# Matrix-LSTM heads in spans of 256 tokens with a chained state, on one core

## The chip, the core and the metric

One core of a Trainium2 chip runs the program. TensorE (PE; PEld is its weight load) multiplies, VectorE (DVE), ScalarE (ACT) and GpSimd (POOL) work on elements, SyncE (SP) issues the loads of weights. The metric is the device time of one execution in microseconds (us).

## The reference

One decoder layer for 1024 tokens, width 1024, all float32. Its first part runs two groups of heads on one input projection, sparse attention (NSA, 8 heads) and the matrix LSTM (mLSTM, 4 heads of 128), then projects both back and adds them to `x`. Cross attention and a gated MLP follow. The change lies in the mLSTM heads:

```python
def step(carry, inp):                       # chunks of 64 tokens
    C, n, m = carry
    qq, kk, vv, ii, lf = inp
    b = jnp.cumsum(lf, axis=-1)
    D = jnp.where(causal, b[..., :, None] - b[..., None, :] + ii[..., None, :], -jnp.inf)
    m_inter = b + m[..., None]
    m_t = jnp.maximum(jnp.max(D, axis=-1), m_inter)
    a_inter = jnp.exp(m_inter - m_t)
    sc = jnp.einsum('bhtd,bhsd->bhts', qq, kk) * jnp.exp(D - m_t[..., None])
    num = a_inter[..., None] * jnp.einsum('bhtd,bhde->bhte', qq, C) + jnp.einsum('bhts,bhse->bhte', sc, vv)
    den = a_inter * jnp.einsum('bhtd,bhd->bht', qq, n) + jnp.sum(sc, axis=-1)
    h = num / jnp.maximum(jnp.abs(den), jnp.exp(-m_t))[..., None]
    ...
```

`q` and `k` come from a causal convolution of four taps and a SiLU; `h` is normalized by head and multiplied by a sigmoid gate `o`.

## The kernel before

Products of float32 matrices are made of three matmuls on split operands (high by high, low by high, high by low: `product`, lines 1066 to 1070). GpSimd splits each 128-column weight tile (`w_hi` L882, `w_lo` L887) once TensorE has begun the tile before, into two slots that take turns. `gemm_tile` projects one tile over 1024 tokens in two halves of 512, each into one of the eight banks of PSUM; a ring gives out the banks as chunks in order, and `open_chunk` waits until the chunk seven before it has been taken out (`chunk_freed`).

After attention come the four mLSTM heads. A head's order on TensorE: projection of q; transposes of the head before (`turn_head`, which waits for `hm_ready`); projections of k, v and the gate; transposes of v (`mv_feat`); the scores of all 36 causal pairs of 128-token blocks in twelve `pieces` of up to 512 columns; in head 3 also the 32 transposes of the attention output `o_nsa`; then the products with v, 1 to 8 for each block of tokens (L1342), into numerator and denominator (129 columns).

VectorE takes q out, convolves it (L2557 to L2562), splits it after ScalarE's SiLU (L2259), multiplies the gate of the head before (L2546), does the same for k, takes v out (L2576), makes the masked exponents of the eight diagonal blocks (L2583), takes the gate out (L2586) and v's tokens (L2589), multiplies each piece of scores by its decay (L2601, L2606; the exponentials are ScalarE's, L1865), takes out the outputs (L2621, L2622) and normalizes the head (L2626 to L2634), which ends in `h_mls`. In head 3 it also makes the low parts of the attention output and of heads 0 to 2 in `h_hi`/`h_lo`, all ahead of the outputs.

Then `mixed` begins the output projection with the first two weight tiles over both token halves; for k from 4 on (the mLSTM heads) it waits for `split_ready`. `turn_head(3)` stands behind 18 groups of three matmuls. Each engine does its instructions in the order of the code.

## Time and profile before

| what | value |
|---|---|
| runs | 1744.65, 1744.93, 1745.40 us, median 1744.93 |
| the profiled execution | span 1742.3 us from first to last instruction |
| busy | TensorE 97%, its weight loads 81%, VectorE 71%, GpSimd 51%, ScalarE 42% |
| mean granted TensorE clock | 0.987 |
| mLSTM heads | 448.5 to 696.1 us of the span |

The page gives the span of one profiled execution and no longer time of it. Matmuls are pipelined: a record's duration is longer than its distance from the next one, so the distance between starts is what a product costs. A float32 product is two records. Columns of instructions in order of time: start, duration, engine, line, operation, output and inputs, shape, count, and in brackets the idle time before with what released it.

### The profile page before, as it was taken

How to read it: one execution, taken by the hardware profiler on the slowest of the kernel's cores; microseconds unless marked ns; L12 is line 12 of the kernel's file. 1: busy time of each engine (PE TensorE's matmuls, PEld its weight loads, DVE VectorE, ACT ScalarE, POOL GpSimd, SP SyncE). 2: the span in 40 equal slices, each digit the busy share in tenths (PEclk: the TensorE clock that was granted, in tenths of full speed). 3: DMA queues.
4: the chain of work that ended last, by engine and by line, in shares of the span. 5: the costliest groups of instructions: out<-in, count | busy, mean ns of one | idle time of the engine just before them, and what ended most of it. 6: DMA issues, size and time to landing. Idle time of an engine off the chain costs nothing.

```text
span 1742.3 us, 23240 instructions
## 1 busy us (share of the span) xinstructions
PE 1682.1 (97%) x8496; PEld 1406.2 (81%) x8496; DVE 1229.0 (71%) x1654; ACT 729.4 (42%) x1367; POOL 881.1 (51%) x671
## 2 busy tenths in 40 slices
PE   7998899998999999999999999999999999999997
PEld 6886788887788888889888787878888888877886
DVE  6764578776777877546554535878888878789965
ACT  5113577876233134115332314343444444443444
POOL 3342345443422421430412544379988788779841
PEclk9999899999999999999999999999999999999999
DMA  5230111110111113224201142234543454685332
GB/s 197 68 103 25 49 33 29 34 29 25 45 41 37 59 38 109 97 97 159 84 25 36 49 145 86 78 121 164 188 157 127 139 167 148 246 297 174 126 124 97
DMA packets 80334, 176.51 MB, mean 101 GB/s; under 512 B 7836, under 2 KB 24412, under 8 KB 80096
## 3 DMA queue, kind: packets, MB, share of 16 engines
q1 hardware_dynamic: 67944, 135.71, 23.5%
q10 hardware_dynamic: 12280, 39.34, 6.0%
q8 instruction: 68, 1.11, 0.3%
q14 instruction: 42, 0.34, 0.1%
HBM read 136.21 MB, written 38.81 MB: 100 GB/s over the span
## 4 chain that ended last, share of the span: by engine, by line
PE 56%; DVE 15%; POOL 12%; ACT 8%; issue 8%; DMA 1%; ACTq 0%; SPq 0%; POOLq 0%; DVEq 0%
PE ps L1066 13%; PE ps L1070 13%; PE ps L1069 13%; DVE x_t L2845 4%; PE ps L1260 3%; POOL sum_s L977 2%; ACT x_t L2086 2%; PE ps L1342 2%; POOL w_lo L971 2%; POOL w_lo L1027 2%; PE ps L1231 2%; PE ps L1281 2%; PE ps L1282 1%; DVE x_t L2874 1%; PE ps L1232 1%
## 5 line engine op out<-in xcount | busy, mean ns | idle before, releaser
L1066 PE MATMUL ps<-h_hi,w_hi 128*128 128x512 f32 x1060 | 418.3, 395 | 8.1 <-POOL h_lo L955 3.2
L1069 PE MATMUL ps<-h_lo,w_hi 128*128 128x512 f32 x1060 | 413.9, 390 | 0.0
L1070 PE MATMUL ps<-h_hi,w_lo 128*128 128x512 f32 x1060 | 413.8, 390 | 0.0
L882 POOL TENSOR_TENSOR w_hi<-w_raw,ones 128x1024 fp32r<-128x1024 f32 x52 | 109.3, 2101 | 516.3 <-PE ps L1066 433.5
L1066 PEld LDWEIGHTS ps<-h_hi,w_hi 128*128 128x128 f32 x1060 | 199.5, 188 | 57.4 <-ACT p_sum L2055 8.5
L1070 PEld LDWEIGHTS ps<-h_hi,w_lo 128*128 128x128 f32 x1060 | 199.5, 188 | 42.2
L1069 PEld LDWEIGHTS ps<-h_lo,w_hi 128*128 128x128 f32 x1060 | 199.6, 188 | 39.6
L915 POOL TENSOR_SCALAR probs<-probs,nsa_inv,gate_sig 128x640 f32<-128x640 f32 (+7 forms) x128 | 100.3, 783 | 178.6 <-DVE nsa_inv L2462 178.6
L2845 DVE SCALAR_TENSOR_TENSOR x_t<-ps,par,x_t 128x1023 f32<-128x1023 f32 x84 | 107.7, 1282 | 72.7 <-ACT x_t L2086 71.2
L2258 DVE TENSOR_TENSOR pt_lo<-ps,pt_hi 128x512 fp32r<-128x512 f32 (+1 forms) x148 | 101.7, 688 | 59.3 <-ACT pt_hi L1796 57.4
L887 POOL TENSOR_TENSOR w_lo<-w_raw,w_hi 128x1024 fp32r<-128x1024 f32 x52 | 139.6, 2685 | 4.0
L1796 ACT ACTIVATE pt_hi<-ps 128x512 fp32r<-128x512 f32 (+1 forms) x148 | 87.8, 596 | 51.7 <-PE ps L1260 51.0
L1260 PE MATMUL ps<-ident,probs 128*128 128x128 f32 (+1 forms) x592 | 97.7, 290 | 11.5 <-POOL probs L915 6.7
L1776 ACT ACTIVATE probs<-ps,nsa_shift 128x640 f32<-128x640 f32 (+7 forms) x128 | 89.7, 701 | 41.4 <-DVE nsa_shift L2450 22.6
L2450 DVE TENSOR_REDUCE nsa_shift<-ps 128x1 f32<-128x640 f32 (+7 forms) x128 | 88.9, 698 | 22.2 <-PE ps L1240 15.7
L1260 PEld LDWEIGHTS ps<-ident,probs 128*128 128x128 f32 (+1 forms) x592 | 66.4, 143 | 25.4 <-issue 11.1
L1231 PE MATMUL ps<-k_a,q_st 128*128 128x512 f32 (+3 forms) x192 | 70.2, 365 | 9.8 <-ACT probs L1776 5.3
L2258 DVE TENSOR_TENSOR z_lo<-h_part,z_hi 128x512 fp32r<-128x512 f32 x40 | 59.1, 1492 | 12.0 <-ACT z_hi L2133 12.0
L971 POOL TENSOR_TENSOR w_lo<-w_raw,w_hi 128x512 fp32r<-128x512 f32 x38 | 52.3, 1377 | 29.9 <-ACT w_hi L2073 29.9
L1281 PE MATMUL ps<-pt_hi,v_hl 128*128 128x512 f32 x132 | 65.3, 495 | 0.0
L1232 PE MATMUL ps<-k_a,q_st 128*128 128x512 f32 (+3 forms) x192 | 65.0, 345 | 0.0
L2686 DVE TENSOR_TENSOR x_t<-ps,x_t 128x1024 f32<-128x1024 f32 x16 | 19.5, 1222 | 64.0 <-PE ps L1070 63.9
(385 smaller groups left out, 4199.6 us busy)
## 6 DMA issues: line engine op xcount, KB each, us to landing
w_raw<-in_w_tiles SPq DMA_DIRECT2D x109, 512.0 KB, 3.4
w_raw<-in_w_tiles SPq DMA_DIRECT2D x55, 256.0 KB, 3.0
s_new<-in_w_tiles SPq DMA_DIRECT2D x44, 256.0 KB, 4.2
z_dram<-x_t ACTq DMA_DIRECT2D x21, 512.0 KB, 2.9
b<-z_dram SPq DMA_DIRECT2D x33, 256.0 KB, 3.8
q_st<-q_dram SPq DMA_DIRECT2D x64, 128.0 KB, 2.9
x_dram<-x_t ACTq DMA_DIRECT2D x14, 512.0 KB, 2.6
t_dram<-t_new ACTq DMA_DIRECT2D x22, 256.0 KB, 5.0
```

The lines of the kernel that those rows point to most:

```text
L882: pool.tensor_tensor(w_hi[s][:, :], w_raw[s][:, :], ones[:, :].to_broadcast([P, KT * P]), ALU.mult).then_inc(w_hi_made.sem, w_hi_made.up())
L887: pool.tensor_tensor(w_lo[s][:, :], w_raw[s][:, :], w_hi[s][:, :].bitcast(FP32), ALU.subtract).then_inc(weights_split.sem, weights_split.up())
L915: ins = pool.tensor_scalar(row, row, nsa_inv[:, j % 8, br:br + 1], gate_sig[:, i, 3 * h + 1 + br:3 * h + 2 + br], ALU.mult, ALU.mult)
L1066: ins = mm(out_ap, whi, x_hi, start=first, stop=False)
L1069: mm(out_ap, whi, x_lo, start=False, stop=False)
L1070: return mm(out_ap, wlo, x_hi, start=False, stop=last)
L1231: mm(o, qa, k_a[br][:, g, at_key:at_key + m], start=True, stop=False)
L1260: last = transpose(ps[0:width, 4 + k % 2, hd * P:hd * P + P], probs[:, at_p:at_p + width], ident[:, :])
L1281: mm(o, v, pt_hi[k % 3][0:e, :], start=br == 0 and a == 0, stop=False)
L1776: ins = f(probs[:, P_AT[j]:P_AT[j] + n], flat[:, 0:n], ACT.Exp, bias=nsa_shift[:, j % 8, br:br + 1], accum_out=nsa_sums[:, j % 8, br:br + 1])
L2258: return tt(out_lo, src, hi.bitcast(FP32), ALU.subtract)
L2845: ins = stt(fc[p][i][:, k:SEQ], ps_flat[:, b:b + SEQ - k], conv_f[:, FTAPS - 1 - k, n:n + 1], fc[p][i][:, k:SEQ], ALU.mult, ALU.add)
```

## The change

A head works in four spans of 256 tokens. Scores are made within a span only (three blocks of 128x128 per span). What lies further back comes through a state: the decayed key tokens `k_tok` times v's tokens, for three spans, and VectorE chains the three (`state`). An output of a block is its own span's products plus q times the state before the span, which ScalarE scales by `past_tok` (`past_faded`) and VectorE adds (`h_sum`). The exponentials of `w_tok`, `fade` and the decays inside a span go ahead of the diagonal ones on ScalarE.

The gate's projection is cut in two: its first half comes ahead of the scores, its second behind v's transposes. v is now taken out behind the eight masked exponents. k gets a buffer of its own (`u_key`), of which six blocks are transposed. In head 3 the attention output is transposed and split by token halves, one on each side of the second gate half, and the splits of heads 0 to 2 by halves too, the second ones behind the outputs. Ahead of attention, the gate rows get one more difference on VectorE (768 tokens), six transposes of 4x128, one copy, and one exponential.

```diff
+SPAN = 2 * P
+SPANS = SEQ // SPAN
+PAST = TT - SPAN // P
+SPLIT_ORDER = [(c, 4 + k) for c in range(2) for k in range(MH - 1)] + [(c, 3 + MH) for c in range(2)]
...
+            def head_states():
+                pe.wait_ge(chunk_freed.sem, chunk_done.value(1))
+                b = open_chunk()
+                for j in range(PAST):
+                    at_col = j // 2 * (MDH + 1)
+                    last = mm(ps[:, b, at_col:at_col + MDH + 1], k_tok[:, j, :], mv_tok[:, j, 0:MDH + 1],
+                              start=j % 2 == 0, stop=j % 2 == 1)
+                last.then_inc(chunk_done.sem, chunk_done.up(2))
+                states_at[0] = chunk_done.n
+            def turn_nsa(c):
+                for k in range(4):
+                    transposes([(o_nsa[:, 4 * c + j, k * P:k * P + P], P, j * P) for j in range(4)])
+            def head_scores(h):
+                silu_done.add(2)
+                pe.wait_ge(silu_done.sem, silu_done.value())
+                for js in ((0, 1, 2, 3), (4, 5)):
+                    transposes([(u_key[:, j * P:j * P + P], P, j % 4 * P) for j in js])
+                pe.wait_ge(qk_ready.sem, qk_ready.next())
+                for z in range(SPANS):
+                    b = open_chunk()
+                    for j, at_col in ((2 * z, 0), (2 * z + 1, 2 * P)):
+                        n = SPAN - P * (j % 2)
+                        ts = slice(P * j, P * j + n)
+                        last = product(ps[:, b, at_col:at_col + n], (mk_hi[:, j * P:j * P + P], mk_lo[:, j * P:j * P + P]),
+                                       mq_hi[:, ts], mq_lo[:, ts], True, True)
+                    last.then_inc(chunk_done.sem, chunk_done.up())
+                pe.wait_ge(chunk_freed.sem, chunk_done.value(3 + SPANS))
+                for q in range(2):
+                    transposes([(mv_feat[:, (4 * q + j) * P:(4 * q + j + 1) * P], P, j * P) for j in range(4)])
+                if h == MH - 1:
+                    turn_nsa(0)
             for h in range(MH):
                 gemm_tile(h_hi, h_lo)
                 if h:
                     turn_head(h - 1)
                 gemm_tile(h_hi, h_lo)
-                gemm_tile(h_hi, h_lo, skip=2)
                 gemm_tile(h_hi, h_lo)
-                pe.wait_ge(chunk_freed.sem, chunk_done.value(4))
-                for q in range(2):
-                    transposes([(mv_feat[:, (4 * q + j) * P:(4 * q + j + 1) * P], P, j * P) for j in range(4)])
-                pe.wait_ge(qk_ready.sem, qk_ready.next())
-                for j, a, e in pieces:
+                gemm_tile(h_hi, h_lo, after_half=lambda: head_scores(h))
+                head_states()
+                if h == MH - 1:
+                    turn_nsa(1)
+                for i in range(TT):
+                    z = i // 2
                     b = open_chunk()
-                    product(ps[:, b, 0:e - a], (mk_hi[:, j * P:j * P + P], mk_lo[:, j * P:j * P + P]),
-                                     mq_hi[:, a:e], mq_lo[:, a:e], True, True).then_inc(
-                                         chunk_done.sem, chunk_done.up())
-                turned = 0
-                if h == MH - 1:
-                    for k in range(4):
-                        for q in range(2):
-                            transposes([(o_nsa[:, 4 * q + j, k * P:k * P + P], P, j * P) for j in range(4)])
-                    turned = 8
-                for i in range(TT):
-                    later = len(pieces) - 1 - pieces.index((i, P * i, min(P * i + HALF, SEQ)))
-                    pe.wait_ge(chunk_freed.sem, chunk_done.value(later + turned + i))
-                    b = open_chunk()
-                    for j in range(i + 1):
-                        last = mm(ps[:, b, 0:MDH + 1], tri[:, tri_at(j, i), :], mv_tok[:, j, 0:MDH + 1],
-                                  start=j == 0, stop=j == i)
+                    if z:
+                        if z < SPANS - 1:
+                            if i % 2 == 0:
+                                pe.wait_ge(state_ready.sem, state_ready.next())
+                        else:
+                            pe.wait_ge(chunk_freed.sem, states_at[0])
+                        mm(ps[:, b, 2 * P:2 * P + MDH + 1], u_conv[:, i * P:i * P + P], state[:, z - 1, 0:MDH + 1],
+                           start=True, stop=True)
+                    if i % 2:
+                        mm(ps[:, b, 0:MDH + 1], tri[:, z, 1, :], mv_tok[:, i - 1, 0:MDH + 1], start=True, stop=False)
+                    last = mm(ps[:, b, 0:MDH + 1], tri[:, z, i % 2 * 2, :], mv_tok[:, i, 0:MDH + 1],
+                              start=i % 2 == 0, stop=True)
                     last.then_inc(chunk_done.sem, chunk_done.up())
...
-                        pe.wait_ge(split_ready.sem, k - 3)
+                        pe.wait_ge(split_ready.sem, SPLIT_ORDER.index((c, k)) + 1)
...
+                act.wait_ge(m_loaded.sem, m_loaded.value())
+                edge = lambda z: m_bc[:, z * SPAN + SPAN - 1:z * SPAN + SPAN]
+                for z in range(SPANS - 1):
+                    f(w_tok[:, 2 * z:2 * z + 2], log_in[:, 2 * z:2 * z + 2, h], ACT.Exp, bias=edge(z)).then_inc(
+                        w_ready.sem, w_ready.up())
+                for z in range(SPANS - 2):
+                    f(fade[:, z:z + 1], edge(z), ACT.Exp, scale=-1.0, bias=edge(z + 1)).then_inc(w_ready.sem, w_ready.up())
+                for z in range(SPANS):
+                    f(decay[:, z, 1, :], m_bc[:, z * SPAN + P:z * SPAN + SPAN], ACT.Exp, bias=log_in[:, 2 * z, h:h + 1]).then_inc(
+                        decay_ready.sem, decay_ready.up())
                 act.wait_ge(diag_ready.sem, diag_ready.next())
-                f(u_conv[:, :], u_conv[:, :], ACT.Exp).then_inc(decay_ready.sem, decay_ready.up())
-                for n, (j, a, e) in enumerate(pieces):
-                    chunk_done.add(1)
-                    a2 = a + P if a == P * j else a
-                    if a2 < e:
-                        if n >= 2:
-                            act.wait_ge(chunk_freed.sem, chunk_done.value(2))
-                        f(decay[n % 2][:, 0:e - a2], m_bc[:, a2:e], ACT.Exp, bias=log_in[:, j, h:h + 1]).then_inc(
-                            decay_ready.sem, decay_ready.up())
-                f(o_gate[:, h, :], o_gate[:, h, :], ACT.Sigmoid).then_inc(gate_done.sem, gate_done.up())
+                f(decay[:, :, 0:3:2, :], decay[:, :, 0:3:2, :], ACT.Exp).then_inc(decay_ready.sem, decay_ready.up())
+                chunk_done.add(6 + 1 + 2 + SPANS + 2 + (2 if h else 0))
+                def high_nsa(c):
+                    for k in range(4):
+                        b = chunk()
...
+                        f(h_hi[:, k, c * HALF:c * HALF + HALF], ps[:, b, :], ACT.Copy,
+                          scale=gains[:, G_HEAD, k:k + 1]).then_inc(hi_ready.sem, hi_ready.up())
+                def high_heads(c):
+                    cs = slice(c * HALF, c * HALF + HALF)
+                    for k in range(MH - 1):
+                        f(h_hi[:, 4 + k, cs], o_gate[:, k, cs], ACT.Copy).then_inc(hi_ready.sem, hi_ready.up())
                 if h == MH - 1:
...
+                    high_nsa(0)
+                    high_heads(0)
+                chunk_done.add()
+                gate_taken = chunk_done.value()
+                chunk_done.add(2)
+                if h == MH - 1:
+                    high_nsa(1)
+                    act.wait_ge(chunk_freed.sem, chunk_done.value())
                     act.dma_start(mem_tok[:, :, :], mem[0, :, :].rearrange("(t p) d -> p t d", p=P)).then_inc(
                         mem_loaded.sem, mem_loaded.up())
-                chunk_done.add(8)
+                chunk_done.add(SPAN // P)
+                for i in range(SPAN // P, TT):
+                    b = chunk()
+                    f(h_sum[:, i, 0:MDH + 1], ps[:, b, 2 * P:2 * P + MDH + 1], ACT.Copy,
+                      scale=past_tok[:, i - SPAN // P, h:h + 1]).then_inc(past_faded.sem, past_faded.up())
+                if h == MH - 1:
+                    high_heads(1)
+                act.wait_ge(chunk_freed.sem, gate_taken)
...
-                b = chunk(2)
-                tt(mv_feat[:, :], both(b), r_in[:, :], ALU.mult).then_inc(chunk_freed.sem, chunk_freed.up(4))
-                chunk_done.add(2)
...
                 for j in range(TT):
                     js = slice(j * P, j * P + P)
-                    ins = stt(u_conv[:, js], m_bc[:, js], log_in[:, j, h:h + 1], mmask[:, :], ALU.add, ALU.min)
+                    ins = stt(decay[:, j // 2, j % 2 * 2, :], m_bc[:, js], log_in[:, j, h:h + 1], mmask[:, :], ALU.add, ALU.min)
                 ins.then_inc(diag_ready.sem, diag_ready.up())
                 b = chunk(2)
-                tt(o_gate[:, h, :], both(b), r_in[:, :], ALU.mult).then_inc(chunk_freed.sem, chunk_freed.up(2))
+                tt(mv_feat[:, :], both(b), r_in[:, :], ALU.mult).then_inc(chunk_freed.sem, chunk_freed.up(2))
+                def take_gate(c):
+                    b, cs = chunk(), slice(c * HALF, c * HALF + HALF)
+                    tt(o_gate[:, h, cs], ps[:, b, :], r_in[:, cs], ALU.mult).then_inc(chunk_freed.sem, chunk_freed.up())
+                take_gate(0)
+                w_ready.add(2 * SPANS - 3)
+                dve.wait_ge(w_ready.sem, w_ready.value())
+                for j, n in ((0, 4), (4, 2)):
+                    b = chunk()
+                    tt(k_tok[:, j:j + n, :], ps[:, b, 0:n * P].rearrange("p (t d) -> p t d", d=P),
+                       w_tok[:, j:j + n, None].to_broadcast([P, n, P]), ALU.mult).then_inc(chunk_freed.sem, chunk_freed.up())
+                decay_ready.add(SPANS + 1)
+                dve.wait_ge(decay_ready.sem, decay_ready.value())
+                for z in range(SPANS):
+                    b = chunk()
+                    tt(tri[:, z, :, :].rearrange("p b t -> p (b t)"), ps[:, b, 0:3 * P],
+                       decay[:, z, :, :].rearrange("p b t -> p (b t)"), ALU.mult).then_inc(chunk_freed.sem, chunk_freed.up())
                 for q in range(2):
                     b = chunk()
                     dve.tensor_copy(mv_tok[:, 4 * q:4 * q + 4, 0:MDH],
                                          ps[:, b, :].rearrange("p (t d) -> p t d", d=P)).then_inc(
                                              chunk_freed.sem, chunk_freed.up())
-                decay_ready.add(1)
-                for n, (j, a, e) in enumerate(pieces):
+                if h == MH - 1:
+                    low_nsa(0)
+                    for k in range(MH - 1):
+                        split_head(0, k)
+                take_gate(1)
+                b = chunk(2)
+                dve.tensor_copy(state[:, 0, 0:MDH + 1], ps[:, b, 0:MDH + 1]).then_inc(state_ready.sem, state_ready.up())
+                for z in range(1, SPANS - 1):
+                    dve.wait_ge(state_ready.sem, state_ready.value())
+                    ins = stt(state[:, z, 0:MDH + 1], state[:, z - 1, 0:MDH + 1], fade[:, z - 1:z],
+                              ps[:, b, z * (MDH + 1):(z + 1) * (MDH + 1)], ALU.mult, ALU.add)
+                    if z < SPANS - 2:
+                        ins.then_inc(state_ready.sem, state_ready.up())
+                ins.then_inc(chunk_freed.sem, chunk_freed.up(2))
+                if h == MH - 1:
+                    low_nsa(1)
+                for i in range(TT):
                     b = chunk()
-                    a2 = a + P if a == P * j else a
...
+                    own = ps[:, b, 0:MDH + 1]
+                    if i < SPAN // P:
+                        ins = dve.tensor_copy(h_sum[:, i, 0:MDH + 1], own)
+                    else:
+                        dve.wait_ge(past_faded.sem, past_faded.next())
+                        ins = tt(h_sum[:, i, 0:MDH + 1], h_sum[:, i, 0:MDH + 1], own, ALU.add)
                     ins.then_inc(chunk_freed.sem, chunk_freed.up())
                 if h == MH - 1:
...
                     for k in range(MH - 1):
-                        split_head(k)
-                for i in range(TT):
-                    b = chunk()
-                    dve.tensor_copy(hv[:, i, :], ps[:, b, 0:MDH]).then_inc(vector_chain.sem, vector_chain.up())
-                    dve.tensor_copy(head_d[:, 0, i:i + 1], ps[:, b, MDH:MDH + 1]).then_inc(
-                        chunk_freed.sem, chunk_freed.up())
+                        split_head(1, k)
                 dve.wait_ge(chunk_freed.sem, chunk_freed.value())
-                chained(stt(head_d[:, 1, :], head_d[:, 0, :], -1.0, head_d[:, 0, :], ALU.mult, ALU.max))
+                den = h_sum[:, :, MDH]
+                chained(stt(head_d[:, 1, :], den, -1.0, den, ALU.mult, ALU.max))
```

## Rows read from the trace of the kernel before

**Rows 1.** The page: its first line, and part 1, busy time, share, instructions.
```profile
span 1742.3 us, 23240 instructions
PE 1682.1 (97%) x8496; PEld 1406.2 (81%) x8496; DVE 1229.0 (71%) x1654; ACT 729.4 (42%) x1367; POOL 881.1 (51%) x671
```

**Rows 2.** Waits of TensorE from 446 to 760: total, times, longest, in us.
```profile
PE ps L1342 <- DVE h_lo L2259: 2.2, 1, 2.2
```

**Rows 3.** Stretches: length, busy time (instructions) by engine, granted clock, DMA share, GB/s.
```profile
572.00:632.00 60.00, 59.96 (x316) 51.38 (x316) 45.54 (x69) 17.38 (x22) 18.82 (x9) 1.00 0.13 45
...
684.00:688.00 4.00, 1.79 (x8) 1.56 (x8) 2.69 (x5) 4.00 (x8) 0.00 (x0) 0.79 0.97 366
688.00:692.00 4.00, 4.00 (x30) 4.00 (x29) 4.00 (x7) 4.00 (x6) 0.00 (x0) 0.78 1.03 417
```

**Rows 4.** TensorE in order of time, heads 0 to 3.
```profile
448.50 0.50 PE L1066 MATMUL ps<-h_hi,w_hi 128*128 128x512 f32 x1 [0.93 <-DVE o_nsa L2475]
...
507.61 0.47 PE L1066 MATMUL ps<-h_hi,w_hi 128*128 128x512 f32 x1
...
552.16 1.04 PE L1108 MATMUL ps<-ident,mv_feat 128*128 128x128 f32 x8
552.95 0.48 PE L1066 MATMUL ps<-mq_hi,mk_hi 128*128 128x512 f32 x1
...
558.95 0.29 PE L1066 MATMUL ps<-mq_hi,mk_hi 128*128 128x256 f32 x1
...
559.32 0.22 PE L1066 MATMUL ps<-mq_hi,mk_hi 128*128 128x128 f32 x1
...
559.60 8.25 PE L1342 MATMUL ps<-mv_tok,tri 128*128 128x129 f32 x72
567.61 0.47 PE L1066 MATMUL ps<-h_hi,w_hi 128*128 128x512 f32 x1
...
627.90 0.47 PE L1066 MATMUL ps<-h_hi,w_hi 128*128 128x512 f32 x1
```

**Rows 5.** TensorE in order of time, end of head 3 and start of mixing.
```profile
679.88 4.12 PE L1108 MATMUL ps<-ident,o_nsa 128*128 128x128 f32 x32
686.21 10.09 PE L1342 MATMUL ps<-mv_tok,tri 128*128 128x129 f32 x72 [2.21 <-DVE h_lo L2259]
696.05 0.48 PE L1066 MATMUL ps<-h_hi,w_hi 128*128 128x512 f32 x1
...
708.39 1.09 PE L1108 MATMUL ps<-ident,h_mls 128*128 128x128 f32 x8
```

**Rows 6.** VectorE in order of time, heads 0 and 1.
```profile
487.57 1.23 DVE L2259 SCALAR_TENSOR_TENSOR mk_lo<-u_conv,mk_hi 128x1024 fp32r<-128x1024 f32 x1 [2.22 <-ACT mk_hi L1855]
...
489.84 2.18 DVE L2583 SCALAR_TENSOR_TENSOR u_conv<-m_bc,log_in,mmask 128x128 f32<-128x128 f32 x8
...
516.73 1.23 DVE L2634 TENSOR_TENSOR h_mls<-u_conv,head_d 128x1024 f32<-128x1024 f32 x1
...
542.80 1.93 DVE L2259 SCALAR_TENSOR_TENSOR mk_lo<-u_conv,mk_hi 128x1024 fp32r<-128x1024 f32 x1 [2.22 <-ACT mk_hi L1855]
544.64 1.21 DVE L2576 TENSOR_TENSOR mv_feat<-ps,r_in 128x1024 f32<-128x1024 f32 x1
545.78 3.19 DVE L2583 SCALAR_TENSOR_TENSOR u_conv<-m_bc,log_in,mmask 128x128 f32<-128x128 f32 x8
...
562.69 0.28 DVE L2621 COPY u_raw<-ps 128x128 f32<-128x128 f32 x1
```

**Rows 7.** GpSimd in order of time, one split in head 1, the last beside head 3.
```profile
543.72 3.26 POOL L887 TENSOR_TENSOR w_lo<-w_raw,w_hi 128x1024 fp32r<-128x1024 f32 x1
...
703.98 3.27 POOL L933 TENSOR_TENSOR first_lo<-w_raw,first_hi 128x1024 fp32r<-128x1024 f32 x1
```

**Rows 8.** ScalarE in order of time, head 1.
```profile
561.58 0.40 ACT L1865 ACTIVATE decay<-m_bc,log_in 128x128 f32<-128x128 f32 x1 [0.49 <-DVE tri L2606]
```

**Rows 9.** VectorE in order of time, end of head 3.
```profile
706.75 1.58 DVE L2634 TENSOR_TENSOR h_mls<-u_conv,head_d 128x1024 f32<-128x1024 f32 x1
```

More of the change, by code:

```diff
@@ L571, in build @@
         rows = lambda g, s=1: slice(DH * g, DH * g + DH)
-        tri_at = lambda j, i: sum(TT - a for a in range(j)) + i - j
-        pieces = [(j, a, min(a + HALF, SEQ)) for j in range(TT) for a in range(P * j, SEQ, HALF)]
         F1 = SEVEN if PLAIN < FT else DOWN
@@ L1172, in _ @@
             b = open_chunk()
[L1173 to L1174 removed]
+            for src, at_col, n in ((g_i, 0, TT), (g_f, 64, TT), (g_t, 128, PAST)):
+                for j in range(n):
                     last = transpose(ps[:, b, at_col + MH * j:at_col + MH * j + MH], src[:, j * P:j * P + P],
@@ L1893, in _ @@
             freed_now()
-            f(h_hi[:, KT - 1, :], o_gate[:, MH - 1, :], ACT.Copy).then_inc(hi_ready.sem, hi_ready.up())
-            act.wait_ge(split_ready.sem, MH)
+            for c in range(2):
+                cs = slice(c * HALF, c * HALF + HALF)
+                f(h_hi[:, KT - 1, cs], o_gate[:, MH - 1, cs], ACT.Copy).then_inc(hi_ready.sem, hi_ready.up())
+            act.wait_ge(split_ready.sem, len(SPLIT_ORDER))
             def square(u, src):
@@ L2638, in _ @@
             dve.wait_ge(chunk_freed.sem, chunk_freed.value())
-            split_head(MH - 1)
+            for c in range(2):
+                split_head(c, MH - 1)
             def residual_loop(turns=KT // 2):
```

102 lines of the change are left out of this document (52 added, 50 removed).

## The prediction

> **What bounds the kernel now.** I read the page first, then waits, stretches and instructions in order of time. The busy shares show TensorE at 97% of the span and nothing else above 81% [rows 1]. From the start of the first mLSTM head to the end of the mixing layer's start, the list of waits has one TensorE wait over 1 us, 2.2 us [rows 2]; the stretch 572 to 632, which is one head, is 59.96 us of TensorE busy out of 60, at full clock [rows 3]. So a microsecond of matmul taken out of a head is a microsecond off the end, unless VectorE becomes late. VectorE is busy 45.54 us of those 60, so it has room on average, and the question is where its chain meets TensorE.
>
> **A head before, on TensorE.** Heads begin at 448.50, 507.61, 567.61 and 627.90 and the last one's products end at 696.05 [rows 4, 5]: periods 59.1, 60.0, 60.3, 68.15. From 507.61 to 552.16 lie four projection tiles and eight transposes of 0.8: 44.55 - 0.8 = 43.75, 10.9 a tile, 5.45 a half. Then 0.8 for the transposes of v, 6.65 for the scores (552.95 to 559.60), 8.0 for the 36 products with v (559.60 to 567.61, 72 records, 0.22 us a product) [rows 4].
>
> **A head after, on TensorE.**
> - Scores: four spans of a 256-wide and a 128-wide group of three. Such groups took 559.32 - 558.95 = 0.37 and 559.60 - 559.32 = 0.28 [rows 4]. 4 x 0.65 = 2.6, so 4.05 less.
> - Outputs: 8 diagonal + 4 neighbour + 6 state products = 18 of 0.22 = 4.0, so 4.0 less.
> - States: 6 products, 1.35 more. Transposes of six key blocks: 0.6 more.
> Sum: 8.05 - 1.95 = 6.1 us less a head, 24.4 for four, if nobody waits.
>
> **Where TensorE meets VectorE inside a head.** Times are from the head's first projection, by head 1 (507.61). Half the gate ends at 0.8 + 3.5 x 10.9 = 39.0; transposes to 39.6. The low part of k is there at 542.80 + 1.93 - 507.61 = 37.1 [rows 6], so the wait for q and k costs nothing in heads 1 to 3. But the fourth score chunk needs a PSUM bank that v's projection holds, and VectorE now takes v out behind the eight masked-decay operations. Those took 3.19 us in head 1 but 2.18 in head 0, where GpSimd was idle [rows 6]; the weight split ran until 543.72 + 3.26 = 546.98 [rows 7], and the first of them stood until then. Before, taking v out (1.21 us) lay in the shadow of that block. Now the eight begin at 37.1, stand until 39.4 and end where they ended before, 548.97, that is 41.4; v follows until 42.6. TensorE wants the bank at 39.6 + 3 x 0.65 = 41.5: a wait of 1.05 us. Bounds: 0 if the masked operations are not held up (they would end at 39.3), 1.3 if v's copy is slow as well. I take 1.05, for the same two instructions stand in the same order in the row. The next two PSUM needs (gate half 43.2 for TensorE at 43.6; first key-token bank 43.9 for 44.1) just fit. Head: 60.0 - 6.1 + 1.05 = 54.9.
>
> Behind that, VectorE has the key tokens (1.1), four decay products on 384 columns (2.0), v's tokens (1.25, two halves near v's own 1.21 [rows 6]) and is done by 47.4, before the second gate half (49.5). The states' chain is three short operations; the nearest row is a 128x128 copy out of PSUM, 0.28 [rows 6]. With the gate half in front they end about 1.2 us after the state products, and the state-free outputs of tiles 0 and 1 give TensorE 0.66 to do; tile 4 and 6 need the later states at +1.8 and +2.9. Cost 0, bounds 0 to 0.5. Each of the six faded copies on ScalarE is near 0.4 (its 128x128 operation, [rows 8]); the last addition lands about 1.0 us after the last product, not 0.6. The normalization's first step stands behind GpSimd until 2.5 us anyway, so the normalized head still comes 10.4 us after the outputs (516.73 + 1.23 - 507.61 [rows 6]) and the turn at 10.9 has 0.5 us left. The sigmoid, now behind the fades, has until the next head's q is split: nothing.
>
> **Head 0** starts VectorE late: k is split at 487.57 + 1.23 = 488.8 [rows 6], while TensorE stands ready at 448.5 + 38.15 + 0.6 = 487.2. Wait 1.6, and then v's bank: 488.8 + 2.2 + 1.2 = 492.2 against 490.8, 1.4. 59.1 - 6.1 + 3.0 = 56.0; gain 3.1. **Heads 1, 2**: 60.0 and 60.3 become 54.9: 5.1 and 5.4.
>
> **Head 3.** The 32 NSA transposes (4.12 us) ran into full banks: a 2.21 us wait, and the 72 records took 10.09 instead of 8.0 because the granted clock fell to 0.79 and 0.78 behind it [rows 3, 5]. Split in two, 16 of them sit ahead of the second gate half. By the ring of eight banks each then finds one: second gate half 46.2 to 51.6, states to 53.0, 16 transposes to 55.1, outputs to 59.1 from the head's start. The wait and its slow clock go. 68.15 - 59.1 = 9.0 gained. Sum up to here: 3.1 + 5.1 + 5.4 + 9.0 = 22.6.
>
> **What is late next: the turn of head 3.** Before, the splits of heads 0 to 2 lay ahead of the outputs. Now their second halves (three operations with two SBUF inputs, about 0.6 each) stand on VectorE between the last addition and the normalization, and GpSimd has four weight operations from 0.6 us after the first mixing product: 1.89, 2.4, 1.89, 2.4, until 703.98 + 3.27 - 696.05 = 11.2 [rows 5, 7]. The two take turns: while the last h_mls operation needs 1.23 in head 1 it took 1.58 here, since it stood until 707.25, the end of the last split operation [rows 6, 7, 9]. In turn: GpSimd to 2.5, split, GpSimd to 5.5, split, to 8.0, split, to 11.0, and only then the normalization, whose steps alone are 0.1 + 0.2 + 0.2 + 1.2 + 1.2 + 1.2 + 0.5 + 1.2 plus gaps = 6.2: ready at 17.2. TensorE wants it at 12.3 (708.39 - 696.05, [rows 5]). Wait: 5.0. Bounds: 0 (nobody stands: splits and normalization end at 9.4) and 5.5. I take 5.0: if VectorE kept its place for all three splits, GpSimd's eight microseconds would stand in the normalization instead, 4.6. A wait of 2.21 us was followed by the low clock [rows 3, 5], so this one is too; 3.4 us at half clock cost 1.7 (the extra of the 72 records was 2.1). The three split_ready waits are met (needed at 7.5, 8.2, 8.9; done at 3.1, 6.1, 8.6).
>
> The Trainium skill, SBUF — State Buffer, section "Who interferes with whom", states the rule that speaks against this move: a VectorE operation with two SBUF inputs and a GpSimd operation that reads SBUF exclude each other for the whole instruction, and whoever issues first has the ports. The stretched rows agree [rows 7, 9]. By its "first issued" alone the order of the three splits is open, which is the difference between my 5.0 and 4.6.
>
> The gate rows ahead of attention (one VectorE operation on 4x768, six tiny transposes, one copy, one exponential) lie where VectorE has idle time ahead of a tile: 0, bounds -0.5 to +1.5, by the later start of attention and its clock. The smaller DVE and ScalarE pieces elsewhere lie under TensorE. The weight loads keep their order.
>
> **Sum.** 22.6 - 5.0 - 1.7 = 15.9 off. The page's execution has a span of 1742.3, and the page gives no longer time for it; the median of the runs is 1744.93, 2.6 more, which I leave as it is. 1742.3 - 15.9 + 2.6 = 1729.0.
>
> **Rivals.**
> - A: no wait at the turn. For it: operations with a PSUM input don't stand, and GpSimd may start its own later. Against: every two-input operation there was stretched before. 1729.0 - 6.7 = 1722.3. Chance 0.22.
> - B: the waits among the scores set off the slow clock in each head. For it: head 0 waits 3.0 in two pieces among short products. Against: 1.05 is half of the only wait that did it here. 4 x 1.7 = 6.8: 1735.8. Chance 0.17.
> - C: VectorE becomes the bound, slower than before. Its place is the span chain of every head: key tokens, decay products, states, additions, normalization, next q. If strided sums and added waits make it 4.0 us late at the turn, TensorE waits 3.5, the clock falls (1.7) and, since k's split follows VectorE, it comes again in every head: 4 x 5.2 = 20.8 more, 1749.8. It decides from 9 us lost beyond my sum in the stage's first head, or 4.0 late in each. Against: 14.5 us of free time a head. Chance 0.05.
> - D: it does half of what it says, since each output waits for a state, a fade or a bank: half of 24.4 stays, 12.2 less gained: 1741.2. Chance 0.06.
> - My own sum: 0.50, with its range 1725 to 1733.
>
> **The numbers.** Range: A's lower edge by -0.5 ahead of attention and no wait among scores in heads 1 to 3 (3 x 1.05): 1719, to B's with the longer bounds: 1737. C and D stay outside (0.11), and some of A and B. A measurement can tell about 0.2%, 3.5 us: faster is below 1741.4. Faster takes my sum, A, B and half of D, less a little for what none of these sees: 0.93. Same 0.02, slower 0.05.
>
> **What would show it.** Right: heads of 54 to 56 us between first projections; a TensorE wait near 1 us among the scores, released by the copy into mv_feat; no wait at the outputs of head 3; a wait of 4 to 6 us at the last h_mls transposes, with splits and normalization stretched by GpSimd, and a low clock behind it. Wrong: that wait missing (A), clock under 1 inside heads 0 to 2 (B), TensorE waiting for h_mls or state in every head (C, D).

## The result and the profile after

The changed kernel takes 1727.01 us (median of 4 runs, 1726.19 to 1727.8) against 1744.79 for the kernel before on the same chip: ratio 0.9899, 95% interval 0.9885 to 0.9912, 17.8 us off. In a later comparison it was 1726.7 against 1742.82, ratio 0.9901 (0.9885 to 0.9918). The predicted time was 1729.0, the range of its own sum 1725 to 1733.

The page of the changed kernel, first line and part 1, answering to [rows 1]:

```profile
span 1725.8 us, 22943 instructions
PE 1661.9 (96%) x8382; PEld 1387.8 (80%) x8382; DVE 1224.5 (71%) x1592; ACT 725.0 (42%) x1388; POOL 880.4 (51%) x671
```

TensorE lost 20.2 us of busy time and the span 16.5: most of what was taken out went straight to the end. VectorE lost only 4.5 of its busy time and keeps 71%. Where the rest went stands in the list of TensorE's waits of the changed kernel from 440 to 760 (total, times, longest), answering to [rows 2]:

```profile
PE ps L1118 <- DVE h_mls L2738: 3.3, 1, 3.3
PE ps L1076 <- DVE mv_feat L2674: 2.4, 4, 0.6
...
PE ps L1076 <- DVE h_sum L2722: 0.6, 1, 0.6
```

The 2.2 us at the outputs of head 3 are gone. New are one wait at the turn of head 3 and a small one among each head's scores. TensorE of the changed kernel in order of time, answering to [rows 4, 5] (start, length, engine, line, operation, count, wait in front):

```profile
447.65 0.80 PE L1076 MATMUL ps<-h_hi,w_hi 128*128 128x512 f32 x1 [0.93 <-DVE o_nsa L2555]
...
491.44 0.39 PE L1076 MATMUL ps<-mq_hi,mk_hi 128*128 128x256 f32 x1 [0.61 <-DVE mv_feat L2674]
...
503.87 0.47 PE L1076 MATMUL ps<-h_hi,w_hi 128*128 128x512 f32 x1
...
558.85 0.47 PE L1076 MATMUL ps<-h_hi,w_hi 128*128 128x512 f32 x1
...
613.83 0.48 PE L1076 MATMUL ps<-h_hi,w_hi 128*128 128x512 f32 x1
...
658.01 1.91 PE L1118 MATMUL ps<-ident,o_nsa 128*128 128x128 f32 x16
...
673.09 0.47 PE L1076 MATMUL ps<-h_hi,w_hi 128*128 128x512 f32 x1 [0.59 <-DVE h_sum L2722]
...
688.90 1.97 PE L1118 MATMUL ps<-ident,h_mls 128*128 128x128 f32 x8 [3.28 <-DVE h_mls L2738]
...
723.82 2.20 PE L1118 MATMUL ps<-ident,mem_tok 128*128 128x128 f32 x16
...
952.13 0.50 PE L1076 MATMUL ps<-h_hi,w_hi 128*128 128x512 f32 x1 [0.31 <-POOL h_lo L965]
```

The distances between first projections are 56.2, 55.0, 55.0 and 59.3, where they were 59.1, 60.0, 60.3 and 68.15. The account against the kernel before, point for point:

| TensorE reaches | before | after | gained so far |
|---|---|---|---|
| first projection of head 0 | 448.50 | 447.65 | 0.85 |
| first product of mixing | 696.05 | 673.09 | 22.96 |
| last h_mls transposes | 708.39 | 688.90 | 19.49 |
| transposes of mem_tok | 740.63 | 723.82 | 16.81 |
| the same product behind h_lo, later in the kernel | 969.26 | 952.13 | 17.13 |
| end of the span | 1742.3 | 1725.8 | 16.5 |

The rows for 740.63 and 969.26, from the kernel before:

```profile
740.63 2.21 PE L1108 MATMUL ps<-ident,mem_tok 128*128 128x128 f32 x16
...
969.26 0.50 PE L1066 MATMUL ps<-h_hi,w_hi 128*128 128x512 f32 x1 [0.32 <-POOL h_lo L955]
```

The first 0.85 can't be laid to an edit: in a second profile of the kernel before, this projection starts at 447.74, 0.76 earlier than in the first, and in a second one of the changed kernel at 447.27. The second profile of the kernel before, starts of heads 0 and 1:

```profile
447.74 0.80 PE L1066 MATMUL ps<-h_hi,w_hi 128*128 128x512 f32 x1 [0.93 <-DVE o_nsa L2475]
...
509.30 0.47 PE L1066 MATMUL ps<-h_hi,w_hi 128*128 128x512 f32 x1
```

So the four heads brought 22.1 us, the turn took 3.5 back, and the stretch from there to the transposes of mem_tok 2.7 more. What lies behind is less steady: from mem_tok to the product behind h_lo the two profiles of the changed kernel need 228.3 and 230.3.

The 22.1 sets unlike clocks against each other. The first products of head 0 ran at full clock in the profile of the kernel before and at the lower level in that of the changed one (a first product of 0.50 us and one of 0.80). In the second profile of the kernel before they ran at the lower level too, head 0 took 61.56 instead of 59.11, and the four heads 250.24 instead of 247.55. Lower level against lower level the four heads brought 24.8 us (250.24 to 225.44), full clock against full clock 22.3 (247.55 to 225.23, in the first kernel of the next section).

Why 2.7 were lost behind the turn is in the granted clock (the number right behind the five busy times with their counts; 1.00 is 2.4 GHz, 0.50 is 1.2 GHz; the columns are those of [rows 3]) of the changed kernel:

```profile
684.00:688.00 4.00, 1.62 (x8) 1.00 (x6) 3.62 (x5) 0.21 (x1) 0.00 (x0) 0.97 0.36 131
688.00:692.00 4.00, 3.10 (x12) 2.81 (x13) 1.88 (x2) 0.00 (x0) 0.00 (x0) 0.50 0.45 148
692.00:696.00 4.00, 4.00 (x14) 3.18 (x13) 1.54 (x3) 2.77 (x5) 0.00 (x0) 0.68 0.62 249
```

The clock falls to the lower level behind the 3.28 us wait and stays there into the third stretch, though TensorE is busy again from 688.90; in [rows 3] it was 0.79 and 0.78 over two stretches behind 2.21 us. Between 688.90 and the first product with first_hi at 702.05 lie 13.15 us, where the kernel before has 10.48 (708.39 to 718.87): that is all of the 2.7.

### The profile page after: what moved, and what is told of

The parts are those of the page before. It is cut to its first block, busy times and chain, and to the rows that moved or that the text cites. A ratio compares the mean times of both kernels' runs of the same rounds, so it can differ in the third digit from the quotient of the medians.

```text
span 1725.8 us, 22943 instructions
## 1 busy us (share of the span) xinstructions
PE 1661.9 (96%) x8382; PEld 1387.8 (80%) x8382; DVE 1224.5 (71%) x1592; ACT 725.0 (42%) x1388; POOL 880.4 (51%) x671
## 4 chain that ended last, share of the span: by engine, by line
PE 53%; DVE 16%; POOL 13%; ACT 8%; issue 8%; DMA 1%; ACTq 0%; POOLq 0%; DVEq 0%; SPq 0%
PE ps L1076 13%; PE ps L1080 12%; PE ps L1079 12%; DVE x_t L2950 4%; PE ps L1270 3%; POOL sum_s L987 2%; ACT x_t L2158 2%; POOL w_lo L981 2%; POOL w_lo L1037 2%; PE ps L1291 2%; PE ps L1241 2%; DVE x_t L2979 1%; POOL spare_lo L1037 1%; PE ps L1292 1%; PE ps L1242 1%
## 5 line engine op out<-in xcount | busy, mean ns | idle before, releaser
L1270 PE MATMUL ps<-ident,probs 128*128 128x128 f32 (+1 forms) x592 | 97.3, 289 | 12.3 <-POOL probs L925 6.7
```

The costliest lines, as they stand in the source:

```text
L1270: last = transpose(ps[0:width, 4 + k % 2, hd * P:hd * P + P], probs[:, at_p:at_p + width], ident[:, :])
```

## The experiments

The theory going in: the turn of head 3 waits because VectorE's three second-half splits and the normalization alternate with GpSimd's four weight operations; the small waits come from v's copy standing behind the masked exponents; everything else is TensorE's own work. The rivals: the turn is late for the length of VectorE's own chain; the waits among the scores hide another wait right behind them; the order of the work in the head (half a gate first, NSA in halves) does nothing. Each kernel below is the changed kernel with one edit, unless it says otherwise. The kernel before had a median of 1746.14 beside the first four and of 1746.08 beside the next four.

### GpSimd's last two weight operations held back

```diff
             split_pairs((FIRST_KV - 11 - KT) // 2 + 1)
+            pool.wait_ge(t("hm_ready").sem, MH)
             split_aside()
```

> The changed kernel, but GpSimd begins the split into first_hi and first_lo only when the fourth head's normalized output is there (one wait more on GpSimd). Theory 1, the shared port: two of VectorE's normalization steps stand behind these two operations, 1.86 and 3.08 us where 0.1 and 1.23 are needed, 3.6 in sum, so the turn's wait of 3.3 us falls under 0.5 and the low clock behind it goes too (2.5): 1727.0 - 5.8 = 1721.2. Rival, the queue on VectorE alone: the three splits ahead of the normalization make it late, their 5.8 us stay, the wait stays over 2.5 and the time within 1 us of 1727.

1722.45 us, ratio 0.9866 (0.9848 to 0.9884). hm_ready is raised when the last h_mls operation is done. The turn no longer waits and the clock stays up. VectorE of this kernel at the end of head 3:

```profile
674.78 5.80 DVE L2331 TENSOR_TENSOR h_lo<-o_gate,h_hi 128x512 fp32r<-128x512 f32 x3 [0.16 <-ACT h_hi L1934]
680.51 0.16 DVE L2731 SCALAR_TENSOR_TENSOR head_d<-h_sum 128x8 f32<-128x8 f32 x1
...
681.15 1.22 DVE L2734 TENSOR_TENSOR u_conv<-h_sum,head_d 128x1024 f32<-128x1024 f32 x1
```

Its GpSimd:

```profile
675.03 2.20 POOL L892 TENSOR_TENSOR w_hi<-w_raw,ones 128x1024 fp32r<-128x1024 f32 x1 [20.51 <-PE ps L1077]
677.31 2.73 POOL L897 TENSOR_TENSOR w_lo<-w_raw,w_hi 128x1024 fp32r<-128x1024 f32 x1
686.70 1.90 POOL L940 TENSOR_TENSOR first_hi<-w_raw,ones 128x1024 fp32r<-128x1024 f32 x1 [6.66 <-DVE h_mls L2739]
```

Its stretches, clock at 1.00 in both:

```profile
684.00:688.00 4.00, 4.00 (x23) 3.35 (x22) 2.43 (x4) 0.21 (x1) 1.30 (x1) 1.00 0.15 19
688.00:692.00 4.00, 4.00 (x20) 3.28 (x19) 3.23 (x3) 1.15 (x2) 3.00 (x2) 1.00 0.91 347
```

The same part of the changed kernel, VectorE:

```profile
673.46 5.79 DVE L2330 TENSOR_TENSOR h_lo<-o_gate,h_hi 128x512 fp32r<-128x512 f32 x3 [0.16 <-ACT h_hi L1933]
679.18 1.86 DVE L2730 SCALAR_TENSOR_TENSOR head_d<-h_sum 128x8 f32<-128x8 f32 x1
...
681.52 3.08 DVE L2733 TENSOR_TENSOR u_conv<-h_sum,head_d 128x1024 f32<-128x1024 f32 x1
```

Its GpSimd:

```profile
673.71 2.20 POOL L892 TENSOR_TENSOR w_hi<-w_raw,ones 128x1024 fp32r<-128x1024 f32 x1 [20.51 <-PE ps L1076]
675.99 2.72 POOL L897 TENSOR_TENSOR w_lo<-w_raw,w_hi 128x1024 fp32r<-128x1024 f32 x1
678.67 2.34 POOL L940 TENSOR_TENSOR first_hi<-w_raw,ones 128x1024 fp32r<-128x1024 f32 x1
681.09 2.42 POOL L943 TENSOR_TENSOR first_lo<-w_raw,first_hi 128x1024 fp32r<-128x1024 f32 x1
```

With first_hi gone the first step of the normalization takes 0.16 instead of 1.86, with first_lo gone the first large one 1.22 instead of 3.08. The three splits stay at 5.80, since w_hi and w_lo are still there. VectorE's own chain is unchanged, so its length was not what made the turn late. From the first product of mixing to the transposes of mem_tok 44.53 us pass (674.41 to 718.94) where the changed kernel needs 50.73: 6.2 less, the 3.5 of the turn and the 2.7 of the clock. (To the later product behind h_lo it is 5.3 less, 273.75 against 279.04, with the unsteady stretch in it.)

### The second-half splits ahead of the outputs

```diff
                 if h == MH - 1:
+                    for k in range(MH - 1):
+                        split_head(1, k)
                     low_nsa(1)
...
                     ins.then_inc(chunk_freed.sem, chunk_freed.up())
-                if h == MH - 1:
-                    for k in range(MH - 1):
-                        split_head(1, k)
```

On ScalarE, high_heads(1) moves ahead of high_nsa(1) likewise, behind one added wait for the gate's second half.

> The changed kernel, but in head 3 the second halves of heads 0 to 2 are split ahead of the attention output's second half instead of behind the outputs, on ScalarE and VectorE. Theory 1: the normalization starts right behind the last addition and stands behind GpSimd as it did before the change, ready 12.3 us after mixing begins, so the turn's wait is under 0.3; the outputs wait about 0.9 us more for banks and additions: 1727.0 - 3.3 - 2.5 + 0.9 = 1722.1. Rival: the 1.9 us of splits only move, the wait shows at the outputs instead with over 2 us and a low clock there: 1726 to 1728.

1723.48 us, ratio 0.9876 (0.9858 to 0.9893). The same three operations, ahead of GpSimd's work, take 1.89 instead of 5.79; VectorE of this kernel:

```profile
669.38 1.89 DVE L2330 TENSOR_TENSOR h_lo<-o_gate,h_hi 128x512 fp32r<-128x512 f32 x3
```

The turn wait goes here too: h_mls is ready 9.9 us after mixing began (the expectation had 12.3), TensorE wants it at 12.4. TensorE pays for it in head 3, which takes 60.87 us instead of 59.26, 1.6 more: a wait of 1.37 for h_sum at the first product of mixing, 0.59 in the changed kernel, and more in the outputs. To the transposes of mem_tok it wins 6.2 (44.54 against 50.73). So the place of the three splits, and of GpSimd's four operations beside them, is the cause of the turn's wait: either of two edits that separate them removes it.

### v's copy ahead of the masked exponents

```diff
+                b = chunk(2)
+                tt(mv_feat[:, :], both(b), r_in[:, :], ALU.mult).then_inc(chunk_freed.sem, chunk_freed.up(2))
                 dve.wait_ge(m_loaded.sem, m_loaded.next())
...
-                b = chunk(2)
-                tt(mv_feat[:, :], both(b), r_in[:, :], ALU.mult).then_inc(chunk_freed.sem, chunk_freed.up(2))
```

> The changed kernel, but VectorE takes v out ahead of the eight masked exponents, as before the change. Theory 1: this copy lies in the shadow of GpSimd's weight split, the fourth score chunk finds its bank, four waits of 0.61 us go: 1727.0 - 2.4 = 1724.6. Rival: the wait is made by the scores' own chunk order and only moves to the next bank (gate half or key tokens): 1726.5 to 1727.5.

1723.19 us, ratio 0.987 (0.9853 to 0.9888). All four waits for mv_feat are gone and nothing takes their place: first projection to mixing 222.49, 2.95 less (the four waits were 2.4), with the first products of head 0 at the lower level in both. The turn is as it was: the list of TensorE's waits of this kernel, 440 to 760, begins with the same line for h_mls as that of the changed kernel, 3.3 us.

### The whole gate projection ahead of the scores

```diff
-                gemm_tile(h_hi, h_lo, after_half=lambda: head_scores(h))
+                gemm_tile(h_hi, h_lo)
+                head_scores(h)
                 head_states()
```

The bank counts and ScalarE's and VectorE's take_gate follow.

> The changed kernel, but the whole gate projection comes ahead of the scores: undoes that part alone. Theory 1: the second gate half covers VectorE's key tokens, decay products and v tokens; without it TensorE waits about 1.4 us ahead of the states in each head and 4 in head 3, where the attention output's low parts lie there too, while the four 0.6 us waits among the scores go: 1727.0 + 4 to 8 = 1731 to 1735. Rival: VectorE is far enough ahead and the half gate is worth nothing: within 1 us of 1727.

1729.99 us, ratio 0.9909 (0.989 to 0.9927). TensorE of this kernel, the states of head 3:

```profile
669.22 2.95 PE L1332 MATMUL ps<-mv_tok,k_tok 128*128 128x129 f32 x12 [2.77 <-DVE h_lo L2332]
```

Its stretches, the clock at 0.57 and 0.58:

```profile
668.00:672.00 4.00, 2.78 (x13) 2.78 (x14) 2.97 (x5) 1.62 (x4) 0.00 (x0) 0.57 1.01 410
672.00:676.00 4.00, 4.00 (x23) 4.00 (x22) 2.93 (x6) 2.49 (x4) 0.00 (x0) 0.58 0.42 165
```

Without the second half of the gate between scores and states, heads 0 to 2 wait 0.9 each for v's tokens, and head 3 waits 2.77 for the NSA split and runs at the low clock behind it. The turn comes 247.91 us after the first projection instead of 241.25: 6.7 us, of which 5.3 in head 3 with its turn, that the half tile behind the scores had hidden. The median is only 3 us worse than the changed kernel's and below the 1731 to 1735 expected; by ratio it is 0.9909 against 0.9899, intervals overlapping. So the runs do not show that the half gate pays. The trace of the stage does (that of the slowest of the four runs, 1735.67), but the size of the whole stays within the noise.

### All NSA transposes together behind the gate

Here turn_nsa(0), high_nsa(0), low_nsa(0) and the first-half splits move behind the second gate half and the states, next to the second ones.

> The changed kernel, but all 32 transposes of the attention output and their splits come behind the second gate half and the states: undoes the halves of the turns alone. Theory 1: eight chunks stand in the ring ahead of the outputs, VectorE needs 5.4 us of low parts and 1.9 of splits for them while TensorE has 4.2 us of transposes, so the outputs wait 2 to 4 us and the clock falls behind it (1.7 to 2); the turn stays at 3 to 4: 1727.0 + 4 to 6 = 1731 to 1733. Rival: the removed work, not the order, freed head 3, so this costs under 1 us: 1726 to 1728.

1731.0 us (2 runs), ratio 0.9917 (0.9895 to 0.9938). TensorE of this kernel:

```profile
672.93 0.49 PE L1381 MATMUL ps<-state,u_conv 128*128 128x129 f32 x2 [1.53 <-DVE h_lo L2329]
...
677.21 0.47 PE L1076 MATMUL ps<-h_hi,w_hi 128*128 128x512 f32 x1 [1.37 <-DVE h_sum L2719]
```

The wait of [rows 5] comes back at the outputs, smaller, and with it the late sum: from the last score group to mixing 19.9 us instead of 16.7. The low clock, which the expectation had behind these two waits, did not come. So of the 9 us that head 3 gained, 3.2 hang on the division of the NSA part in two, and here without the clock's share.

### The gate rows alone

The kernel before with only the added rows ahead of attention (four-row subtraction, six more transposes).

> The kernel before with only the additions to the gate rows ahead of attention on VectorE and TensorE (one difference, six transposes, the negation moved ahead of them). Theory 1: they lie in idle time, attention's first scores begin within 0.7 us of the kernel before (140.4 for 139.8 as in the changed kernel), and the end moves by under 1 us. Rival: the later start shifts the low clock in attention and the first head by more, 1.5 us or more either way.

> The kernel before, looked at once more. Theory: the stage of attention ends at times that differ by 1 to 2 us between looks, since the low clock there falls at other places, so the changed kernel's start of the first head, 0.85 us ahead of the one in the first look, is no effect of the change: here between 447.5 and 449.5. The four heads take 247.5 within 0.5. Rival: attention ends at 448.5 within 0.2 whenever the program is the same.

One run of 1746.78 with the rows, one of the kernel before of 1743.29, where the runs of the kernel before on this chip go from 1743.19 to 1748.74: two single runs 3.5 us apart show nothing within that spread. The first product of attention's scores behind a wait comes at 139.65 us with the rows, at 139.77 in the first profile of before and 139.17 in the second: the rows move it by no more than 0.5. In the two profiles of the changed kernel it comes at 140.43 and 140.19, 0.4 to 1.3 later. The changed kernel also has a copy and an exponential there, which this kernel lacks, and what those cost was not tested; what the additions cost at the end stays open.

One expectation for the kernel before failed. Its four heads were to take 247.5 within 0.5, and took 250.24, with 2.45 of the 2.69 in head 0, where its first products ran at the lower clock. The kernel with the rows has the same: 250.10.

### Both edits

The first and the third edit in one kernel.

> The changed kernel with v taken out ahead of the masked exponents and GpSimd's split into first_hi and first_lo behind the fourth head's normalized output. Theory: the two gains add, since one lies in the four heads and one behind them; against the changed kernel 2.9 us less from its first projection to the start of mixing, 5.3 us less from there to the end of the key projections: 1727.0 - 8.2 = 1718.8, range 1717 to 1721. Rival: the first gain only shifts where the clock falls and where later waits stand, and the sum is under 6: 1721 or more.

> The version with the copy into mv_feat ahead of the masked exponents and GpSimd's first_hi/first_lo held until h_mls is ready, on the same chip as the changed kernel. Theory: 7 to 9 us faster than the changed kernel (turn wait 3.3, its low clock 2.5, four bank waits 2.4), ratio to before 0.985. Rival, the difference of 7.8 us between medians of different chips is half noise: 3 to 5 us.

> The changed kernel unchanged, beside the version with both edits, on the same chip. So far the two were compared only through the kernel before. Theory: the wait of 3.3 us at the last h_mls transposes with a low clock behind it and four waits of 0.6 us for mv_feat belong to the program and come again; ratio to before 0.990, some 17.5 us off. Rival: part of the 17.8 us was the state of one chip; then the ratio is under 0.987 or over 0.993. Whether the start of head 0 has the low clock again is open: about 1.5 us either way.

1719.19 us, ratio 0.9848 (0.9833 to 0.9864). Then it ran beside the changed kernel on one chip: 1718.27 (1717.71 to 1719.21) against 1726.7 (1724.09 to 1728.03), 8.4 us less. Its time is below that of both kernels. TensorE's waits of this kernel from 440 to 760, without those at attention's end:

```profile
PE ps L1077 <- DVE mk_lo L2332: 1.3, 1, 1.3
...
PE ps L1077 <- DVE h_sum L2723: 0.6, 1, 0.6
PE ps L1119 <- DVE o_gate L2680: 0.4, 1, 0.4
```

Its TensorE at the turn, without a wait:

```profile
683.08 1.03 PE L1119 MATMUL ps<-ident,h_mls 128*128 128x128 f32 x8
```

The turn comes 12.36 us after the first product of mixing (670.72), which is when TensorE wants it. From the first projection to the transposes of mem_tok the single edits took 2.95 and 6.2 out of the trace, 9.15 together; both in one kernel take 9.2 (276.17 to 266.98). They add up, and the runs side by side show 8.4 of it. The second profile of the changed kernel gave the same list of waits, 3.3 for h_mls and 0.6 four times for mv_feat.

## The prediction, step by step

**A head on TensorE: right.** 6.1 us less work a head and one bank wait gave 54.9; the trace has 55.0 twice. With v's copy moved the four waits go and the stage gets shorter by 2.95, so nothing else stood right behind them. The pieces fit as well: six key transposes take 0.57 (predicted 0.6), the states 1.33 (1.35).

**v's bank wait: right place and cause, size 0.6 instead of 1.05.** VectorE of the changed kernel, head 1:

```profile
539.06 1.92 DVE L2331 SCALAR_TENSOR_TENSOR mk_lo<-u_key,mk_hi 128x1024 fp32r<-128x1024 f32 x1 [2.22 <-ACT mk_hi L1903]
540.90 4.33 DVE L2671 SCALAR_TENSOR_TENSOR decay<-m_bc,log_in,mmask 128x128 f32<-128x128 f32 x8
545.15 1.21 DVE L2674 TENSOR_TENSOR mv_feat<-ps,r_in 128x1024 f32<-128x1024 f32 x1
```

As predicted the eight operations stand until w_lo is through (539.98 and 3.26 on GpSimd, 543.24) and end at 545.23, 41.4 after the head's first projection at 503.87; v's copy follows until 42.5. Both are to a tenth the predicted times. The fault is on TensorE's side: it came to the bank at 41.9 instead of 41.5, since three spans of scores took 2.3 us, not 3 x 0.65.

**Head 0: right total, wrong way.** 56.0 was predicted, with waits of 1.6 for k and 1.4 for v's bank; 56.2 came, with one wait of 0.61. What stands in their place is the clock. At the head's start:

```profile
447.00:451.00 4.00, 3.35 (x8) 2.67 (x9) 3.79 (x2) 1.42 (x2) 2.40 (x1) 0.50 0.00 0
```

TensorE's first products ran at the lower level; its first tile ended later, so GpSimd's next split, which TensorE releases, began at 461.27, 3.9 us behind VectorE's start on o_nsa. VectorE and GpSimd of the changed kernel:

```profile
457.42 4.91 DVE L2607 TENSOR_TENSOR o_nsa<-o_nsa,rstd 128x512 f32<-128x512 f32 x8
...
461.27 2.81 POOL L892 TENSOR_TENSOR w_hi<-w_raw,ones 128x1024 fp32r<-128x1024 f32 x1 [4.97 <-PE ps L1076]
```

VectorE and GpSimd of the kernel with GpSimd's last two operations held back, where that split began at 460.66, only 1.7 us behind:

```profile
458.95 8.81 DVE L2608 TENSOR_TENSOR o_nsa<-o_nsa,rstd 128x512 f32<-128x512 f32 x8
...
460.66 1.94 POOL L892 TENSOR_TENSOR w_hi<-w_raw,ones 128x1024 fp32r<-128x1024 f32 x1 [2.84 <-PE ps L1077]
```

In this second kernel the clock at this place is 1.00, the eight operations take 8.81, and the two predicted waits are there. Its edit lies 200 us further on and is not the reason: the same two cases, clock at the lower level with 4.91 and full clock with 8.81, are the two profiles of the kernel before. Its TensorE:

```profile
489.53 0.38 PE L1077 MATMUL ps<-mq_hi,mk_hi 128*128 128x256 f32 x1 [1.31 <-DVE mk_lo L2332]
...
492.76 0.39 PE L1077 MATMUL ps<-mq_hi,mk_hi 128*128 128x256 f32 x1 [0.95 <-DVE mv_feat L2675]
```

Its first projection to mixing takes 225.23, the changed kernel's 225.44. In the changed kernel the low clock cost head 0 about what the spared waits would have (56.22 against 56.02), so in this profile the term of 3.0 held by luck: two waits that did not come, and a clock that was not in the sum.

**Head 3: right.** 59.1 predicted, 59.3 measured. The 16 transposes sit at 658.01 without a wait, the outputs run through at full clock. What the sum had at nothing is the start of mixing, which waits 0.59 us for an addition into h_sum. The prediction had the last addition land 1.0 after the last product; it did not follow up that the first product of mixing needs a bank that such an addition frees.

**The gain at mixing: 22.6 predicted, 22.1 measured**, with unlike clocks in head 0. With full clock in both, which is the case that the prediction worked out, it is 22.3; with the lower level in both 24.8.

**The turn: right mechanism, 3.3 instead of 5.0**, and so outside the 4 to 6 that the prediction gave as a sign of being right. The kernel before had no time to spare here: its h_mls was done at 708.33 [rows 9] and TensorE wanted it at 708.39 [rows 5]. The step that was off is the taking of turns. The rows of the changed kernel under the first experiment show another start and another end than the four turns to 11.0 with all of the normalization behind them. VectorE began its first split at 673.46, before GpSimd at 673.71, so one split was free and GpSimd's four were done 10.4 after mixing began. And the three small steps of the normalization were through by 681.48, while first_lo had only begun at 681.09, so only the 5.3 us from u_conv on came behind: ready at 15.8, not 17.2. TensorE wanted it at 12.5.

That each side stands for a whole operation of the other is also what the Trainium skill, SBUF — State Buffer, section "Who interferes with whom", says: an exclusive lock, to whoever issues first. The trace agrees, 2.20 and 2.72 on GpSimd where 1.89 and 2.40 stand alone.

**The clock behind the turn: 2.7 instead of 1.7.** The one sample before had two partly slow stretches; here the transposes themselves ran at the low level (1.97 for eight, 1.03 at full clock in the last kernel).

**The rest.** The state chain costs nothing visible, as predicted; what the additions ahead of attention cost stays open. 22.1 - 3.5 - 2.7 = 15.9, the predicted sum to a tenth, and that is luck in part: the heads fell short by 0.5 and the clock cost 1.0 more, which the turn, 1.5 cheaper, made up. The 0.85 of an earlier first projection makes 16.8 at mem_tok; the end has 16.5, and waits late in the kernel differ by more than that even between the two profiles of the changed kernel (for w_lo 0.7 in sum against 2.5).

The medians differ by 17.8 where the spans differ by 16.5. Every run on record whose span is listed took 1.7 to 1.8 us longer than its span. So the 2.6 between the profiled span of the kernel before and the median was not the page's fixed difference: that execution was some 0.8 us quicker than the median of its kernel, and the profiled one of the changed kernel, 1727.55, was 0.5 slower than its own. That accounts for the 1.3. With 1.7 in place of 2.6 the prediction's sum would have been 1728.1.

**The rivals.** A (no wait at the turn) did not happen, but its time came true once GpSimd was held back: 1722.45 against its 1722.3, with a loss of 6.2 removed where it had priced 6.7. The line against A, that every two-input operation there had been stretched, overstates: in the kernel before, four of the five two-input steps of the normalization were (1.87, 3.07, 2.80 and 1.58 us), and the second took 0.17. B (low clock in each head) fell: 0.61 among the scores, and 1.31 and 0.95 with GpSimd held back, left the clock at 1.00. C and D fell with the periods of 55.

## What to carry to other kernels

When a change makes room on the bound engine, follow the next engine's queue operation by operation through the place where its pieces now land: the loss of the turn, the bank wait and their remedies were all readable from rows of the kernel before. Where VectorE operations with two SBUF inputs meet GpSimd work without a deadline, give the GpSimd work one semaphore that keeps it out of the critical stretch: one line took 6.2 us out of the trace of this stage, and the median was 4.6 us lower. And a copy that frees a PSUM bank goes ahead of work that only needs to be done sometime: two lines moved brought 3.

## What the runs showed of the hardware

Whether the clock falls is not told by the wait's length alone. Waits of 2.21, 2.66, 2.77 and 3.28 us on TensorE had the lower level behind them, 1.53 and 1.37 had not. Nor does the length tell the cost. From the last h_mls transposes to those of mem_tok 32.2 us pass where nothing waits; behind the turn's wait it was 2.7 more in both profiles of the changed kernel (wait 3.3), 1.65 more with the NSA transposes together (3.2), and 1.5 more with the whole gate ahead of the scores (3.9).

At the end of attention all twelve profiles have the same three waits, 0.78 or 0.79, 0.78 and 0.93. In seven of them the first product of head 0 then takes 0.79 or 0.80 us, its length at the lower level, in five 0.50. The two profiles of the kernel before are one of each kind, so this goes by the execution and not by the program. Both of the changed kernel had the lower level there and all three that held GpSimd back had not, but that edit acts 200 us later, and the kernel with the NSA transposes together had full clock as well. What decides it, these traces don't show.

A slower clock can be free. In those seven profiles the eight VectorE operations on o_nsa take 4.90 or 4.91 us, in the other five 8.80 or 8.81, since a slower TensorE releases GpSimd's next split later: 3.9 to 4.2 us behind VectorE's start on them instead of 1.7 to 1.8. In the changed kernel, where head 0 waits for VectorE, this pays for the clock: 56.2 against 56.0. In the kernel before, where head 0 waits for nothing, the lower level costs 2.45: 61.56 against 59.11.
